# Retention: where the block sums of a Strassen-like product are made, and how the gates are spread

## The reference, cut to what matters

```python
proj = einsum('bld,dc->blc', h, w_in)          # rq, rk, rv, rg of a head: 4 x 128 columns
scores = einsum('bnihd,bnjhd->bnhij', qc, kc) * dmask
inner  = einsum('bnhij,bnjhe->bnihe', scores, vc)
kv     = einsum('bnjhd,hj,bnjhe->bnhde', kc, zeta, vc)
state  = g_chunk * state + kv                  # block after block
cross  = einsum('bnihd,hi,bnhde->bnihe', qc, xi, prev)
ret    = head_norm(inner + cross) * silu(rg)
```

## Time and profile before

| | us |
|---|---|
| three timed runs | 3023.16, 3026.87, 3027.12 |
| median | 3026.87 |
| the profiled execution, its own time | 3008.36 |
| its span | 3006.5 |
| mean granted TensorE clock | 0.993 |
| PE busy | 2904.0 (97%) |
| DVE busy | 1389.7 (46%) |
| POOL busy | 1125.0 (37%) |
| ACT busy | 628.5 (21%) |

### The profile page before, as it was taken

How to read it: one execution, slowest core, us unless ns; L and a number is a source line. 1 busy time by engine, 2 the same in 40 slices (tenths; PEclk the granted TensorE clock), 3 DMA queues, 4 the chain that set the end, 5 groups by cost and what they waited for, 6 DMA issues and landing times.

```text
span 3006.5 us, 39111 instructions
## 1 busy us (share of the span) xinstructions
PE 2904.0 (97%) x14184; PEld 2011.8 (67%) x14184; DVE 1389.7 (46%) x3918; ACT 628.5 (21%) x1277; POOL 1125.0 (37%) x1080
## 2 busy tenths in 40 slices
PE   8999998989999999998999999999999999999997
PEld 4478887874445555555455677777777777777765
DVE  6465656562006666675477644233333333233326
ACT  2222111110004455454111100111111111111114
POOL 3533534320000101011145434555555555555535
PEclk9999999999999999999999999999999999999999
DMA  6500110103000011200643466888899999999996
GB/s 223 170 5 1 30 44 1 29 15 114 14 14 3 12 49 54 71 10 30 240 162 120 137 235 200 259 265 262 261 276 271 274 276 287 294 303 306 316 267 248
DMA packets 181009, 462.00 MB, mean 154 GB/s; under 512 B 26072, under 2 KB 98600, under 8 KB 155080
## 3 DMA queue, kind: packets, MB, share of 16 engines
q1 hardware_dynamic: 133872, 339.23, 31.9%
q0 software_dynamic: 44640, 111.84, 16.2%
q10 hardware_dynamic: 2304, 8.39, 0.7%
HBM read 345.44 MB, written 113.92 MB: 153 GB/s over the span
## 4 chain that ended last, share of the span: by engine, by line
PE 50%; POOL 1%; DMA 1%; DVE 1%; issue 0%; ACT 0%; SPq 0%; POOLq 0%; DVEq 0%; ACTq 0%
PE ps L2695 24%; PE ps L2636 11%; PE ps L2495 7%; PE ps L2551 2%; PE ps L2633 2%; PE ps L2561 1%; PE ps L2514 1%; POOL moe_fin L2290 1%; PE ps L2505 0%; DMA base_rows<-moe_yo,index 0%; PE ps L2482 0%; PE ps L2584 0%; DMA moe_fin<-base_rows 0%; PE ps L2535 0%; DVE moe_xT L1852 0%
## 5 line engine op out<-in xcount | busy, mean ns | idle before, releaser
L2208 POOL DMA_INDIRECT moe_xg<-t_rows,index x433 | 416.6, 962 | 166.3 <-issue 125.5
L2695 PEld LDWEIGHTS ps<-moe_xT,moe_wg 128*128 128x128 f32 x2048 | 352.9, 196 | 44.0 <-issue 34.2
L2695 PE MATMUL ps<-moe_xT,moe_wg 128*128 128x192 f32 (+22 forms) x2048 | 378.3, 338 | 0.0
L2695 PE MATMUL ps<-moe_xT,moe_wu 128*128 128x192 f32 (+22 forms) x2048 | 375.3, 336 | 0.0
L2695 PEld LDWEIGHTS ps<-moe_xT,moe_wu 128*128 128x128 f32 x2048 | 353.4, 196 | 4.3
L2636 PE MATMUL ps<-moe_wd,moe_hh 128*128 128x512 f32 (+12 forms) x800 | 353.9, 592 | 0.0
L2229 POOL DMA_INDIRECT base_rows<-moe_yo,index x100 | 164.9, 1649 | 368.0 <-DVE moe_yo L1866 281.8
L1171 POOL TENSOR_TENSOR fox_diag<-fox_c,fox_causal 128x128 f32<-128x128 f32 x128 | 55.7, 457 | 658.8 <-DVE fox_mx L1200 647.6
L1852 DVE STREAM_TRANSPOSE moe_xT<-moe_xg 128x256 f32<-128x256 f32 x433 | 235.4, 607 | 71.6 <-DMA moe_xg<-t_rows,index 71.1
L1752 DVE TENSOR_TENSOR moe_hh<-moe_sl,ps 128x256 f32<-128x256 f32 (+19 forms) x144 | 53.3, 370 | 460.0 <-ACT moe_sl L2349 459.8
L2636 PEld LDWEIGHTS ps<-moe_wd,moe_hh 128*128 128x128 f32 (+12 forms) x800 | 142.3, 180 | 169.0 <-issue 168.8
(11 more groups left out here) (284 smaller groups left out, 4255.3 us busy)
## 6 DMA issues: line engine op xcount, KB each, us to landing
moe_wg<-in_we_gate SPq DMA_DIRECT2D x64, 1024.0 KB
moe_wu<-in_we_up SPq DMA_DIRECT2D x64, 1024.0 KB
moe_wd<-in_we_down SPq DMA_DIRECT2D x64, 1024.0 KB, 8.4
fox_c<-ck SPq DMA_DIRECT2D x8, 1032.0 KB, 8.7
emb_xin<-in_x SPq DMA_DIRECT2D x16, 512.0 KB, 4.3
h_rows<-emb_hr SPq DMA_DIRECT2D x16, 512.0 KB, 2.8
ret_w<-in_w_in SPq DMA_DIRECT2D x16, 512.0 KB, 6.6
moe_yt<-h_rows SPq DMA_DIRECT2D x16, 512.0 KB, 4.8
```

The costliest lines, as they stand in the source:

```text
L2208: pool.indirect_dma_start(out=xg[g % NXG][:, :], out_offset=None, in_=quarters, in_offset=bass.IndirectOffsetOnAxis(ap=route.index4[:, AT4 ...
L2695: ins = pe.matmul(out, w[:, c, f:FF:FC], xT[u][:, c, 0:n], start=(c == 0), stop=(c == DC - 1))
```

## The change

The sums leave GpSimd. `weight_sums` takes any engine, and `token_sums` becomes `token_sum`, which makes one of the four sums. In the embedding VectorE makes head 0's weight sums and unit 0's token sums behind its eviction of the tile (`rest(i)`). In retention VectorE makes the four sums of the next unit one at a time, one step ahead instead of two: before `sum_two`, before the first rotation, behind `sum_four`, and before the second rotation. One weight sum of the next head is made in each of the steps 3 to 6, behind `follow`. GpSimd's loop in retention is only `norm(h)` for each head. The gate pairs are one per step in steps 1 to 7, behind the state update of the second block, and an eighth in step 7 ahead of its first token sum.

```diff
 (embedding)
-                if 9 <= i < 13:
-                    weight_sums(pool, ahead, 0, i - 9)
-                if i == 13:
-                    pool.wait_ge(hT_a, 3)
-                    pool.wait_ge(hT_d, 3)
-                    token_sums(pool, ahead, hT, 0)
             whole_row(NT - 1)
...
                 rest(i)
+                if 9 <= i < 13:
+                    weight_sums(dve, ahead, 0, i - 9)
+                if i == 13:
+                    dve.wait_ge(hT_a, 3)
+                    dve.wait_ge(hT_d, 3)
+                    for x in range(4):
+                        token_sum(dve, ahead, hT, 0, x)
...
 (retention, GpSimd)
-            token_sums(pool, ahead, hT, 1)
-            for U, (h, j) in enumerate(STEPS):
-                if U < 2:
-                    continue
-                pool.wait_ge(proj, after(*STEPS[U - 2], THIRD))
-                token_sums(pool, ahead, hT, U)
-                if j == 2 and h >= 1:
-                    norm(h - 1)
-                if j in (4, 5) and h + 1 < RH:
-                    weight_sums(pool, ahead, h + 1, 2 * (j - 4))
-                    weight_sums(pool, ahead, h + 1, 2 * (j - 4) + 1)
-            norm(RH - 1)
+            for h in range(RH):
+                norm(h)
...
 (retention, VectorE)
+            def next_sum(U, part):
+                if U + 1 < len(STEPS):
+                    if part == 0 and U >= 1:
+                        dve.wait_ge(proj, after(*STEPS[U - 1], THIRD))
+                    token_sum(dve, ahead, hT, U + 1, part)
+
             for U, (h, j) in enumerate(STEPS):
                 if U >= 1:
                     ph_, n0, n1 = before(U)
...
                     mask(ph_, n0)
                     update(ph_, n0 + 1)
+                if h >= 1 and j == UNITS - 1:
+                    gate_pair(h - 1, j - 1)
+                next_sum(U, 0)
                 sum_two(U)
                 if U >= 1:
                     stats(ph_, n0)
                 if j == 0:
                     rotate_meta(h)
                 lead(U)
+                next_sum(U, 1)
                 rotate_block(U, 0)
                 sum_three(U)
-                if h >= 1 and 3 <= j < 7:
-                    gate_pair(h - 1, 2 * (j - 3))
                 values(U, 1)
                 sum_four(U)
+                next_sum(U, 2)
                 if U >= 1:
                     mask(ph_, n1)
                     if n1 + 1 < NX:
                         update(ph_, n1 + 1)
+                if h >= 1 and j >= 1:
+                    gate_pair(h - 1, j if j == UNITS - 1 else j - 1)
                 follow(U)
+                if 3 <= j < 7 and h + 1 < RH:
+                    weight_sums(dve, ahead, h + 1, j - 3)
+                next_sum(U, 3)
                 rotate_block(U, 1)
                 if U >= 1:
                     stats(ph_, n1)
-                if h >= 1 and 3 <= j < 7:
-                    gate_pair(h - 1, 2 * (j - 3) + 1)
```

More of the change, by code:

```diff
@@ L214, with weight_sums @@
 HEAD_PRODUCTS = 1 + PRODUCTS * UNITS
-def weight_sums(pool, ahead, h, part):
+def weight_sums(eng, ahead, h, part):
     u, k, n = h % 2, DC // 2, 2 * RD
@@ L222, in weight_sums, with token_sum @@
     if part == 0:
-        pool.wait_ge(ahead.ret_w[u], h // 2 * 80 + 80 + START)
-        pool.tensor_tensor(t[:, 0, :, :], b12, b11, ALU.subtract).then_inc(made, 1)
+        eng.wait_ge(ahead.ret_w[u], h // 2 * 80 + 80 + START)
+        eng.tensor_tensor(t[:, 0, :, :], b12, b11, ALU.subtract).then_inc(made, 1)
     if part == 1:
-        pool.wait_ge(made, 4 * h + 1)
-        pool.tensor_tensor(t[:, 1, :, :], b22, t[:, 0, :, :], ALU.subtract).then_inc(made, 1)
+        eng.wait_ge(made, 4 * h + 1)
+        eng.tensor_tensor(t[:, 1, :, :], b22, t[:, 0, :, :], ALU.subtract).then_inc(made, 1)
     if part == 2:
-        pool.wait_ge(made, 4 * h + 1)
-        pool.tensor_tensor(b12, b12, b22, ALU.subtract).then_inc(made, 1)
+        eng.wait_ge(made, 4 * h + 1)
+        eng.tensor_tensor(b12, b12, b22, ALU.subtract).then_inc(made, 1)
     if part == 3:
-        pool.wait_ge(made, 4 * h + 2)
-        pool.tensor_tensor(t[:, 2, :, :], b21, t[:, 1, :, :], ALU.subtract).then_inc(made, 1)
-def token_sums(pool, ahead, hT, unit):
+        eng.wait_ge(made, 4 * h + 2)
+        eng.tensor_tensor(t[:, 2, :, :], b21, t[:, 1, :, :], ALU.subtract).then_inc(made, 1)
+def token_sum(eng, ahead, hT, unit, part):
     k, s, made = DC // 2, ahead.tsum[unit % 2], ahead.tsum_set
@@ L241, in token_sums @@
     a11, a12, a21, a22 = hT[:, 0:k, t0:t1], hT[:, k:DC, t0:t1], hT[:, 0:k, t1:t1 + P], hT[:, k:DC, t1:t1 + P]
[L242 to L247, removed]
+    if part == 0:
+        eng.tensor_tensor(s[:, 0, :, :], a21, a22, ALU.add).then_inc(made, 1)
+    if part == 1:
+        eng.tensor_tensor(s[:, 2, :, :], a21, a11, ALU.subtract).then_inc(made, 1)
+    if part == 2:
+        eng.wait_ge(made, 4 * unit + 1)
+        eng.tensor_tensor(s[:, 1, :, :], s[:, 0, :, :], a11, ALU.subtract).then_inc(made, 1)
+    if part == 3:
+        eng.wait_ge(made, 4 * unit + 3)
+        eng.tensor_tensor(s[:, 3, :, :], a12, s[:, 1, :, :], ALU.subtract).then_inc(made, 1)
 def flat(ap):
```

## The result

The changed kernel takes **2985.69 us** (median of four runs, 2983.66 to 2987.97), beside 3026.2 before (four runs, 3023.16 to 3027.12): 40.5 us less, a ratio of 0.9868 with a 95% interval of 0.9851 to 0.9885. It was run again later (e8): 2988.20 beside 3025.71, 0.9874 (0.9858 to 0.9889).

What follows compares the result with a forecast made beforehand. TensorE, busy 97%, bounds the kernel; 49.3 us are lost around it. Less new losses of 17.6 (retention), 0.3 (embedding) and 1.7 (clock), the gain is 29.7: 2997 us, own range 2986 to 3007, whole range 2974 to 3013.

Steps and rivals of the forecast that it cites:

- What bounds it: Whole kernel: TensorE, busy 97%; 39.8 us lost in retention, 32.4 us standing at the outer product, and 9.5 in the embedding.
- The duration of the sums: On VectorE: a 128x512 token sum takes 0.67 us and costs 0.59; a weight sum costs 1.10.
- The rival that had the sums no faster on VectorE: Retention and embedding: sums keep 1.27 and 2.35 us on VectorE, stalls of 62 us, kernel slower at 3047; chance 0.07.
- The walk through a step: Retention: VectorE's lateness beyond 0.85 us to spare stalls TensorE 0.84, 0.3 or 1.4 us by step kind; together 17.6.
- The mask: Retention, ahead of the state update: the mask comes 0.59 us later; nothing taken, 0.2 a step for the range.
- The embedding: From the tenth tile on: turns 7.74 us apart again, 9.5 us loss recovered except 0.3 for the four token sums.
- The rival that kept the embedding's loss: Embedding: GpSimd's row additions and VectorE's sums block each other, 9.2 us stay lost, gain 20.5, time 3006; chance 0.10.
- The gates and the store over the steps: Retention, steps 1 to 7: the root is ready before the first gate and the later store release is hidden; no cost.
- the loss of head 0: Retention's head 0, without gates, was taken as holding almost no loss; about 1 us allowed in the range.
- the clock: After the change: 22 smaller stalls, allowed one stretch of low clock costing 1.7 us.

Runs made afterwards that it cites:

- e8: The changed kernel run again, beside e7 on the same chip; 2988.20 us beside 3025.71 for the kernel before, ratio 0.9874.
- e7: Changed kernel with weight sums moved ahead of lead and gate pairs moved behind sum_three; 2972.48 us beside 3025.71 for the kernel before, ratio 0.9822.
- e4: Changed kernel with one more 128x512 subtraction on VectorE in each step, ahead of the fourth token sum; one run 2985.74 us beside 3013.43 before.
- e2: Kernel before with only the gate pairs placed as in the change, all sums staying on GpSimd; 2974.39 us beside 3013.43, ratio 0.9868.
- e3: Kernel before with gates placed as in the change and embedding's sums on VectorE, retention's sums on GpSimd; 2965.04 us beside 3013.43, ratio 0.9839.

## Why the prediction was right, point by point

The time of 2997 for 2985.69 was in the whole range (2974 to 3013), but 0.3 us below the forecast's own, 2986 to 3007. The gain was under-estimated, 29.7 for 40.5 us timed and 34.8 in the traces. The 5.1 between 29.7 and 34.8 are 1.8 in head 0, 1.6 in heads 1 and 2, 0.4 in head 3 and 1.7 for the clock, less 0.4 in the embedding.

- **What bounds it**: right. The stalls at the outer product went from 32.4 to 11.4 us, and removing the rest (e7) left none.
- **The duration of the sums**: right. 128x512 took 0.68 us (0.67 said) and is followed after 0.60 (0.59 said), e.g. L251 at 354.50 and the rotation at 355.11 behind it; a weight sum is 1.22 and 1.13 (1.18 and 1.10 said). The rule of the Trainium skill ("VectorE: DVE Perf Modes", section on the TRN2 errata) gives an estimated 0.69 and 1.22 for the durations, which this trace confirms; as a cost with no overlap it would have been 0.09 too high each time. The rival that had the sums no faster on VectorE is out.
- **The walk through a step**: right. Weight sum alone 0.84 said, 15.16 - 14.32 = 0.84 measured; gate alone 0.3 said, 0.23; both 1.4 said, 1.36. As waits of TensorE's at the outer product the trace shows less, 0.61, none and 1.13, since some 0.23 of each lies at the load. e4 tested the slack from the other side.
- **The mask**: no wait of TensorE's at L998 beyond the one at the very end of retention, so nothing taken was right. Two waits for the mask of 0.75 us that the kernel before had, in the first gating step of heads 1 and 2, are gone.
- **The embedding**: 9.2 said, 8.8 measured; the late turn stood 0.61, where 0.3 was said for the token sums. (A late turn in tiles 10 to 14 also stood among the signs of being wrong, against the walk's own 0.3; it came, and cost no more than this.) Of the 8.8, 1.7 are the stretch of low clock that went with the last late turn. The rival that kept the embedding's loss is out, although the waiting that it named is there, in both directions: it fits into the time before the turn is due.
- **The gates and the store over the steps**: hidden, as said; neither the root nor the store shows in TensorE's waits.
- **Mis-sized: the loss of head 0.** I set the heads' losses against head 0 and called that almost without loss. It held 1.7 us (118.27 in e7), and one of the 13 waits in the earlier trace rows was in its first step: its first step went from 14.70 to 13.45, and its steps with GpSimd's weight sums had 0.24 too much each. As the measure for heads 1 and 2 it hid 0.5 in each as well.
- **Mis-sized: the clock.** I allowed one low stretch (1.7 us) for 22 small stalls and there was none; and the timed runs of before seem to hold more of them than the profile I summed.
- **A slip in a rival's price.** In the one with the sums no faster on VectorE, the third token sum would make L839 0.24 us late in steps without a gate too; its 62 us lack some 2.4. Nothing else hangs on it.
- **What the prediction did not ask**: which half of the change pays in retention. I priced the departure of the sums and the new places of the gates as one. e2 shows that the places alone bring 34.2 us up to the last step. The change's 34.8 are 8.8 of the embedding and 26.0 of retention (its first sum 8.8 earlier, its last 34.8), so there the sums' move, on top of the gates' places, cost 8.2 us (9.9 without the 1.7 of low clock in e2). Against e3, which has the same embedding, the last step is 9.8 later (637.81 against 628.05). The stalls say why: 11.4 us in 12 waits where e2's four leave 5.4, and 14.9 us at the loads where e2 has 4.9.

## What to carry to other kernels

When two engines hold each other up, look for the moments at which they meet before moving work from one to the other: here a new place for eight small pairs of instructions a head gained as much as the whole change, which also took all the sums away. When an engine works in order, its busy share says little; walk the one chain that ends in the late hand-over, count what lies between its two fixed points, and put movable work outside them. And profile the old kernel twice where its clock varies: a difference of two single traces can be several us off.

## What the runs showed of the hardware

- GpSimd waits for VectorE as VectorE waits for GpSimd. A scaling of one column, 0.22 us otherwise, took 1.20 beside a VectorE sum with both inputs in SBUF (L371 above). VectorE's scaling of the gates, with one large input, also stood: 2.57 us for 0.60. Not every GpSimd instruction does it: beside its power of 128x16 (2.93 us, from 442.04 in the trace of before) VectorE's rotation, also with both inputs in SBUF, took its usual 0.29 at 443.91.
- Up to the end of retention the low clock began only during or right behind stalls of 2.0 us or more in these traces, and not each time. e4's 23 waits of up to 1.7 us drew none (1.00 in the heads shown), nor did those of the changed kernel in both profiles (up to 1.1). The 2.8 us of the kernel before drew a different number in each of three profiles (head 1: 134.40, 139.12 and 132.77 us); e2's head 1, with stalls of 2.0, read 0.99, and its head 2 1.00 with the same stalls.
